# Eight neighbouring weight rows per partition: the load layout of the expert gate and up weights

## The reference

```
t = h.reshape(B * L, D)                       # D = 1024
g_sel = argmax(softmax(t @ w_rg))             # one of 4 groups
wt, idx = top_k(softmax(le_sel), 2)           # two of its 4 experts
for e in range(16):
    a = silu(t @ w_eg[e]) * (t @ w_eu[e])     # gate and up: 1024 -> 512
    y = y + gate[:, e:e+1] * (a @ w_ed[e])    # down: 512 -> 1024
```

## Time and profile before

| | |
|---|---|
| median of 3 runs | 753.33 us (750.51 to 754.04) |
| profiled execution, whole | 752.38 us |
| its span, first to last instruction | 750.6 us |
| TensorE busy | 682.0 us (91%) |
| VectorE, ScalarE busy | 489.9 us, 420.3 us |
| bytes moved | 197.54 MB, mean 263 GB/s |
| issues of gate and up quarters | 64 and 64 (60 and 4), of 512 KB each |

### The profile page before, as it was taken

One profiled execution on the slowest core, in us unless ns is written; L12 is line 12 of the kernel. 1 busy time (PEld: TensorE's weight loads), 2 busy tenths in 40 slices (PEclk: granted clock), 3 DMA queues, 4 the chain that ended last, 5 costly groups with the idle time before them and its releaser, 6 DMA issues.

```text
span 750.6 us, 10815 instructions
## 1 busy us (share of the span) xinstructions
PE 682.0 (91%) x3523; PEld 537.7 (72%) x3523; DVE 489.9 (65%) x694; ACT 420.3 (56%) x626; POOL 72.6 (10%) x120
## 2 busy tenths in 40 slices
PE   3899999999999998989974969999999999999894
PEld 1466556579899986757864858888888888877651
DVE  2546433226554655664458858999999999888938
ACT  4542222224343545775343348887888888888833
POOL 1020101129400000000000600000000000000050
PEclk9899999999999998999975979999999999999988
DMA  9935666659952240300427599999999999999883
GB/s 338 387 132 196 225 225 204 213 165 359 400 160 89 75 141 27 113 1 15 183 74 263 224 347 398 398 398 398 399 398 398 398 398 398 398 398 398 348 301 147
DMA packets 92759, 197.54 MB, mean 263 GB/s; under 512 B 7811, under 2 KB 21176, under 8 KB 92724
## 3 DMA queue, kind: packets, MB, share of 16 engines
q1 hardware_dynamic: 81200, 163.08, 59.5%
q0 software_dynamic: 8224, 25.61, 9.2%
q10 hardware_dynamic: 3302, 8.43, 2.8%
HBM read 166.64 MB, written 30.44 MB: 263 GB/s over the span
## 4 chain that ended last, share of the span: by engine, by line
PE 62%; DMA 14%; DVE 8%; ACT 5%; SPq 4%; issue 4%; POOL 2%; POOLq 0%; ACTq 0%; DVEq 0%
PE ps L1652 14%; PE ps L1463 8%; PE ps L1672 7%; PE ps L1513 6%; PE ps L1499 6%; DMA raw_ring<-in_w_exp_down 5%; PE ps L1500 4%; PE ps L1393 3%; PE ps L1361 3%; DMA raw_ring<-in_w_in 2%; DMA qkv_mem<-in_w_exp_gate 2%; DVE split_ring L1147 2%; PE ps L1554 2%; PE ps L1529 2%; SPq L422 2%
## 5 line engine op out<-in xcount | busy, mean ns | idle before, releaser
L1652 PE MATMUL ps<-split_ring,split_rows 128*128 128x512 f32 x768 | 179.9, 393 | 1.3 <-DVE split_ring L1147 1.3
L1147 DVE TENSOR_TENSOR split_ring<-qkv_mem,split_ring 128x1024 fp32r<-128x1024 f32 x128 | 148.8, 1219 | 26.1 <-ACT split_ring L789 25.5
L1652 PEld LDWEIGHTS ps<-split_ring,split_rows 128*128 128x128 f32 x768 | 143.1, 188 | 31.7 <-DVE split_ring L1147 2.7
L789 ACT CAST split_ring<-qkv_mem 128x1024 fp32r<-128x1024 f32 x128 | 127.0, 1054 | 17.8 <-ACT catT_mem L813 9.3
L1499 PE MATMUL ps<-split_rows,split_ring 128*128 128x384 f32 x288 | 87.7, 345 | 0.8 <-DVE catT_mem L1065 0.4
L1672 PE MATMUL ps<-split_ring,split_rows 128*128 128x512 f32 x360 | 85.6, 393 | 0.0
L1500 PE MATMUL ps<-split_rows,split_ring 128*128 128x256 f32 x288 | 80.5, 279 | 0.0
L1147 DVE TENSOR_TENSOR split_ring<-raw_ring,split_ring 128x1024 fp32r<-128x1024 f32 x64 | 75.3, 1220 | 2.6 <-ACT split_ring L789 2.0
L1672 PEld LDWEIGHTS ps<-split_ring,split_rows 128*128 128x128 f32 x360 | 66.5, 188 | 13.1
L1463 PE MATMUL ps<-split_ring,split_rows 128*128 128x512 f32 x288 | 70.0, 396 | 0.0
L907 DVE TENSOR_TENSOR split_ring<-raw_ring,split_ring 128x1024 fp32r<-128x1024 f32 (+1 forms) x36 | 39.6, 1102 | 44.0 <-ACT split_ring L579 43.5
(11 more groups left out here) (282 smaller groups left out, 877.5 us busy)
## 6 DMA issues: line engine op xcount, KB each, us to landing
qkv_mem<-in_w_exp_gate SPq DMA_DIRECT2D x64, 512.0 KB, 12.3
qkv_mem<-in_w_exp_up SPq DMA_DIRECT2D x60, 512.0 KB, 11.1
raw_ring<-in_w_exp_down SPq DMA_DIRECT2D x60, 512.0 KB, 10.7
raw_ring<-in_w_mod SPq DMA_DIRECT2D x32, 512.0 KB, 4.9
expert_rows<-work POOLq DMA_DIRECT2D x54, 256.0 KB, 9.5
qkv_mem<-in_w_mod SPq DMA_DIRECT2D x16, 512.0 KB, 11.4
catT_mem<-expert_rows SPq DMA_DIRECT2D x16, 512.0 KB, 12.8
expert_rows<-catT_mem ACTq DMA_DIRECT2D x15, 512.0 KB, 6.6
```

Of the source, the lines that this page charges most:

```text
L789: nc.scalar.copy(spl[:, moe_split_slot(tile, j, r), 0, :], moe_raw(tile, j, r)).then_inc(S["hi"], 1)
L1147: tt(spl[:, slot, 1, :], moe_raw(tile, j, r), spl[:, slot, 0, :].bitcast(F32), ALU.subtract).then_inc(S["lo"], 1)
L1652: ins = mm(ps[:, j, :], xS[:, s, k, :], spl[:, slot, m, (k % 2) * N:(k % 2 + 1) * N], start=(k == 0 and s + m == 0), stop=(k == KC - 1 and ...
```

## The change

```
-    w_eg = a["w_exp_gate"].rearrange("l e (k p) n -> (l e) p k n", p=P)
-    w_eu = a["w_exp_up"].rearrange("l e (k p) n -> (l e) p k n", p=P)
+    w_eg = a["w_exp_gate"].rearrange("l e (p k) n -> (l e) p k n", p=P)
+    w_eu = a["w_exp_up"].rearrange("l e (p k) n -> (l e) p k n", p=P)
...
                 for k in range(KC):
-                    ins = nc.tensor.transpose(ps[:, 2 + k // 4, (k % 4) * P:(k % 4 + 1) * P], xtile[p][:, k * P:(k + 1) * P], ident[:, :])
+                    ins = nc.tensor.transpose(ps[:, 2 + k // 4, (k % 4) * P:(k % 4 + 1) * P], xtile[p].rearrange("s (p k) -> s k p", k=KC)[:, k, :], ident[:, :])
...
-                    ins = mm(ps[:, 2 + k // 4, (k % 4) * P:(k % 4 + 1) * P], h2[:, b, k * P:(k + 1) * P], oneh[:, b, :],
+                    ins = mm(ps[:, 2 + k // 4, (k % 4) * P:(k % 4 + 1) * P], h2[:, b, :].rearrange("s (p k) -> s k p", k=KC)[:, k, :], oneh[:, b, :],
```

## The result

Twenty runs of each kernel gave a median of 760.24 us after (755.11 to 763.89) and 753.26 us before. The ratio is 1.0088 with an interval of [1.0071, 1.0105]: slower, by 7.0 us. The forecast was 751.0 us, no change that could be told from none; its range, up to 764.5, held the time. The profiled execution took 761.83 us, 9.45 more than the one of before.

What follows compares the result with a forecast made beforehand. The prediction took DMA to pace the late expert tiles, TensorE close behind. Profiled 752.38 - 2.23 (loads) + 0.4 (transposes) + 0 (selection) = 750.5 us, 751.5 applied to the median; it predicted 751.0, range 748.5 to 764.5.

Steps and rivals of the forecast that it cites:

- What bounds the kernel: Expert tiles: DMA needs 0.75 us more per tile than TensorE, buffers hide about twelve tiles, DMA costs 2.23 us.
- Part 1, loads: Gate and up loads: 4 KB packets raise the rate to 413 GB/s, TensorE stops waiting for weights, 2.23 us gained.
- Part 2, transposes: L1640: step of 8 lengthens the load from 141 to about 190 ns, mostly hidden, 0.4 us in all.
- Part 3, the selection: First tile's L1714, 80 loads with a step of 8: bounds 0 and 3.1 us, taken as 0.
- upper bound of 8.9: L1714: if each load took the whole pace twice, the selection would take 20.3 in place of 11.4 us.
- The first rival: Strided load becomes TensorE's bound: 14.0 us at the transposes, 0 to 3.1 at the selection; 764.2 to 767.3 us, chance 0.15.
- The cover: Idle time ahead of the second tile, TensorE 8.51 us and VectorE 5.78, expected to hide a longer selection.
- The total: Whole kernel: 752.38 - 2.23 + 0.4 + 0 = 750.5 us profiled, 751.5 applied to the median; 751.0 predicted.
- each load taking twice the pace at either level: L1714 at half and full clock: 11 loads before the clock rises in place of 22, then 69 x 0.224 us.

Runs made afterwards that it cites:

- dma_only: All gate and up loads in the new layout, L1714 and the transposes reading neighbouring columns as in the kernel before; 752.17 us, ratio 0.9974 to the kernel before.
- tr_only: The kernel before with only the transposes of L1640 strided by 8; 753.21 us, ratio 1.0004 to the kernel before.
- after_third: The changed kernel itself, timed a third time beside its own runs of the kernel before; 757.38 us, ratio 1.0055.
- first_old: The changed kernel with the first tile's loads and L1714 put back to the old layout; 751.18 us, ratio 0.9963 to the kernel before.
- step4: The kernel before, all layouts old, with L1714 reading every fourth column (16 bytes apart); one run, 755.04 us beside 752.44.
- after_cover: The changed kernel with VectorE's slot arithmetic and second one-hot matrices moved ahead of four first-tile and next-tile steps; 751.74 us, ratio 0.9987 to the kernel before.
- step2: The kernel before, all layouts old, with L1714 reading every second column (8 bytes apart); one run, 752.65 us beside 752.44.
- pairs: A third layout against the kernel before: 4 KB loads with two neighbouring weight rows per partition, tokens read with a step of 2; 753.36 us, ratio 1.0005.

## Why the prediction failed, step by step

- **What bounds the kernel: right.** DMA paced the late tiles, and its whole price was 2.23 us (3 us in the second trace of before).
- **Part 1, loads: right.** Packets, 411 to 413 GB/s (estimate 413), pace and waits came as written; dma_only gives 0.9974, about 2 us. Runs 16 KB apart cost nothing that shows.
- **Part 2, transposes: right.** 192 ns of load (guessed 192), 0.5 us in all by the trace of tr_only (0.4).
- **Part 3, the selection: this is the step that failed**, in the sentence "I take 0: an extra like that of part 2 (51 ns on 80 loads is 4.1 us even unhidden) stays under the cover". The extra was 144 ns of load and 127 ns of pace, and it was not hidden: 7.8 us, near the upper bound of 8.9. I had carried the extra over from another kind of instruction, the transpose, whose load had slack ahead of it (141 ns where 192 hides). L1714's own row already stood at the edge: 192 ns of load, 112 of pace. The first rival named exactly this ("at L1714, with loads of 192 ns, the pace has begun to rise") but priced the binding at the transposes, and took 0 to 3.1 us for the selection only on top of it. That the two could part, hidden in one and bound in the other, was no case of mine. With the upper half of my own bound, 2 to 3 us, the sum would have been 752.5 to 753.5.
- **The cover: right in size, incomplete behind it.** 7.8 - 5.78 = 2.0 us is what tile 1 was late. Not foreseen: the idle time moved next to tile 1 and brought the half clock into it, 0.9 us more. TensorE's own cover even grew: the scatter that it had waited for ended 3.6 us sooner beside the longer selection (last section), so that VectorE's work alone was late.
- **The total.** 752.38 - 2.2 + 0.5 + 2.0 + 0.9 = 753.6, and 0.9 behind the tiles gives 754.5; five of the seven traces of after are executions of 754.6 to 756.2 us, though the medians of three of the four sets lie higher (757.38, 757.44 and 760.24). The first set's 760.24 is not explained by any step: its profiled execution has 3.1 us more than before ahead of the selection, and behind its start 4.35 us more than after_third (2.9 with the late semaphore, 1.4 in the landing of the last write). The late semaphore came in no other trace; a landing as long came once more, in first_old. So the failed step is shown in kind and place, and by the traces in size; of the first set's 7.0 us most stays unexplained.

The page "Advanced Engine Details and Errata" of the Trainium skill, section Memory Cachelines, says that at least two accesses to a line of 16 bytes are needed to absorb the latency of the memory. By that rule two values (step 2) should be free, and one value (step 4 or 8) should pay. The traces agree for L1714: 197, 329 and 336 ns of load, where step 1 has 192. They do not agree for the transposes, where step 2 (209 ns) is the dearer one.

## What to carry over

Price a strided stationary operand at each instruction that reads it, from that instruction's own slack: a step of 8 values was almost free where the load had room and doubled the pace where it had none. The load's growth is not to be carried over either; it was 51 ns at one instruction and 144 at the other. Where a cost falls into idle time, look at what the idle time then stands next to: used-up cover moved the wait, and the half clock with it, into the next tile. A gain of 0.3% is safe only if nothing off the path is made 7.8 us longer; here the first tile could keep its old layout, or VectorE's order could be changed, and either took the loss away.

## What the hardware showed beyond this

- **The strided load has nearly the same pace at either clock.** Two stretches of after_third at the two levels (the clock is the third number from the end):

```profile
410.00:412.00 2.00, 2.00 (x10) 2.00 (x10) 1.71 (x9) 0.00 (x0) 0.00 (x0) 0.50 0.00 0
414.00:416.00 2.00, 2.00 (x10) 2.00 (x10) 1.73 (x10) 0.00 (x0) 0.00 (x0) 1.00 0.00 0
```

Ten matmuls stand in 2 us in both. Before, it was 11 at the half clock and 21 at the full one. (A stretch also counts matmuls that reach into it. From start to start it is 240 ns at the half clock and 238 at the full one; before, 213 and 112.) So my picture of each load taking twice the pace at either level was wrong as well: at the half clock the step costs 27 ns of 213.

- **GpSimd's scatter is slowed by one kind of VectorE's work.** The ten scatters of L524 (issue time in ns, min/median/max) in the kernel before:

```profile
L524 POOL DMA_INDIRECT expert_rows<-catT_mem,slot_index x10: 950/1012/1967, 416.1 to 431.2; - x10
```

And in after_third:

```profile
L524 POOL DMA_INDIRECT expert_rows<-catT_mem,slot_index x10: 948/952/1046, 416.5 to 427.9; - x10
```

In the kernel before, VectorE's splits of the weights stand in the middle of the scatters:

```profile
420.75 4.62 DVE L1147 TENSOR_TENSOR split_ring<-raw_ring,split_ring 128x1024 fp32r<-128x1024 f32 x4
425.29 4.62 DVE L1147 TENSOR_TENSOR split_ring<-qkv_mem,split_ring 128x1024 fp32r<-128x1024 f32 x4
```

The issues that start at 421.23, 423.10, 425.37 and 427.63 us take 1.56, 1.97, 1.96 and 1.97 us; those ahead of 421 and behind 429.9 take 0.95 to 1.04, though VectorE is busy with small operations beside the first of them. In after_third L1147 starts at 429.13, behind the last scatter, and no issue takes more than 1.05 us; in step4 and after_cover it is the same. The last scatter starts 3.6 us sooner from the selection's start (19.4 for 23.0), and the scattered rows are no longer what the first transposes wait for. In step2 and pairs, whose selection is only 0.6 to 0.7 us slower, L1147 starts as much later and three issues are slow in place of four. The last scatter starts 0.6 us sooner from the selection's start, and tile 1 starts at 33.0 and 33.4, where five traces with the fast selection and VectorE's old order have 34.1 to 34.6. A slightly slower selection went with an earlier second tile; the scatters' start times account for 0.6 us of that. That L1147's work slows the issues fits all traces; no run changed it alone.
